# Attention scores of a transformer trunk: the distance term moves from a VectorE pass into TensorE's accumulation

## What is computed

```python
slopes = exp2(-8.0 * arange(1, 9) / 8)                     # one per head
dist = abs(qpos[:, None] - key_pos[None, :])
allowed = (key_pos[None, :] // 64) <= (qpos[:, None] // 64)
bias = where(allowed, -slopes[h] * dist, -inf)
s = einsum('bqhcd,bkhcd->bhcqk', q_blk, k)                 # 64 channels per map
p = softmax(s + bias, axis=-1)
a = p[:, :, 0] - lam_full * p[:, :, 1]
o = einsum('bhqk,bkhe->bqhe', a, v)
```

## Time and profile before

| | value |
|---|---|
| median of three executions | 1612.39 us |
| the profiled execution, its own time | 1613.23 us |
| its span, first to last instruction | 1611.4 us |
| mean granted TensorE clock over the span | 0.973 of full speed |
| head stage, first scores to the first matmul of the output projection | 132.07 to 168.89 us |

### The profile page before, as it was taken

How to read it: one execution, slowest core, us unless ns; L and a number is a source line. 1 busy time by engine, 2 the same in 40 slices (tenths; PEclk the granted TensorE clock), 3 DMA queues, 4 the chain that set the end, 5 groups by cost and what they waited for, 6 DMA issues and landing times.

```text
span 1611.4 us, 21780 instructions
## 1 busy us (share of the span) xinstructions
PE 1493.7 (93%) x9526; PEld 1091.1 (68%) x9526; DVE 472.5 (29%) x1003; ACT 161.5 (10%) x428; POOL 37.6 (2%) x84
## 2 busy tenths in 40 slices
PE   4997999999999899989999999999898899998997
PEld 3864587885477677443356887778683597886884
DVE  1577327351047455151211111111112311011113
ACT  2005210000020121021000000000000000000000
POOL 1000100000011100010000000000000000000000
PEclk8999999999999999999989999999999999999998
DMA  9996129859432110759998999999999999999995
GB/s 336 387 393 230 57 93 366 320 188 360 156 105 105 53 52 1 274 196 357 401 370 337 392 395 392 395 393 395 393 382 398 389 378 395 392 395 392 395 392 202
DMA packets 205824, 483.49 MB, mean 300 GB/s; under 512 B 4241, under 2 KB 6698, under 8 KB 205714
## 3 DMA queue, kind: packets, MB, share of 16 engines
q1 hardware_dynamic: 205106, 481.46, 79.9%
q10 hardware_dynamic: 608, 0.47, 0.1%
HBM read 480.86 MB, written 1.05 MB: 299 GB/s over the span
## 4 chain that ended last, share of the span: by engine, by line
PE 74%; DMA 13%; DVE 5%; SPq 4%; issue 3%; ACT 1%; POOL 0%; DVEq 0%; POOLq 0%
PE ps L1209 18%; PE ps L1729 15%; PE ps L1196 10%; DMA ring<-in_moe_w_gate 7%; PE ps L1787 7%; PE ps L1745 4%; PE ps L1585 3%; DMA ring<-in_moe_w_down 3%; DMA ring<-in_attn_w_in 3%; SPq L620 2%; PE ps L1752 2%; PE ps L1253 2%; PE ps L1635 2%; PE ps L1797 2%; SPq L617 1%
## 5 line engine op out<-in xcount | busy, mean ns | idle before, releaser
L1209 PE MATMUL ps<-hT,ring 128*128 128x256 f32 x1472 | 326.7, 382 | 5.1 <-issue 1.8
L1209 PEld LDWEIGHTS ps<-hT,ring 128*128 128x128 f32 x1472 | 278.6, 191 | 49.0 <-issue 6.5
L1729 PE MATMUL ps<-arena,ring 128*128 128x208 f32 (+1 forms) x1792 | 295.7, 327 | 6.7 <-DMA ring<-in_moe_w_gate 6.7
L1729 PEld LDWEIGHTS ps<-arena,ring 128*128 128x128 f32 x1792 | 292.8, 191 | 9.5 <-DMA ring<-in_moe_w_gate 9.0
L1196 PE MATMUL ps<-ring,arena 128*128 128x512 f32 x368 | 158.8, 592 | 1.3 <-DVE arena L2243 1.3
L1787 PE MATMUL ps<-arena,ring 128*128 128x208 f32 (+1 forms) x896 | 149.3, 327 | 2.6 <-DMA ring<-in_moe_w_down 2.6
L1787 PEld LDWEIGHTS ps<-arena,ring 128*128 128x128 f32 x896 | 145.2, 190 | 3.7 <-DMA ring<-in_moe_w_down 3.0
L1745 PE MATMUL ps<-ring,arena 128*32 128x256 f32 x1792 | 110.2, 401 | 30.6 <-issue 30.6
L1196 PEld LDWEIGHTS ps<-ring,arena 128*128 128x128 f32 x368 | 69.5, 190 | 87.2 <-issue 87.2
L1745 PEld LDWEIGHTS ps<-ring,arena 128*32 128x32 f32 x1792 | 62.7, 116 | 76.2 <-issue 46.1
L2034 DVE SCALAR_TENSOR_TENSOR arena<-ring,cond,arena 128x512 f32<-128x512 f32 x140 | 105.3, 752 | 5.0
(11 more groups left out here) (348 smaller groups left out, 1089.5 us busy)
## 6 DMA issues: line engine op xcount, KB each, us to landing
ring<-in_moe_w_down SPq DMA_DIRECT2D x56, 2048.0 KB, 19.3
ring<-in_moe_w_gate SPq DMA_DIRECT2D x55, 2048.0 KB, 19.4
ring<-in_moe_w_up SPq DMA_DIRECT2D x55, 2048.0 KB, 20.0
ring<-in_mod_w SPq DMA_DIRECT2D x24, 2048.0 KB, 17.0
ring<-in_mlstm_w_in SPq DMA_DIRECT2D x8, 2048.0 KB, 9.1
ring<-in_attn_w_in SPq DMA_DIRECT2D x6, 2048.0 KB, 19.9
ring<-in_ffn_w_gate SPq DMA_DIRECT2D x5, 2048.0 KB, 12.4
ring<-in_ffn_w_up SPq DMA_DIRECT2D x5, 2048.0 KB, 12.8
```

Source lines behind the costliest of these rows:

```text
L1209: ins = pe.matmul(dst, w[:, k, c * P:(c + 1) * P], hT[:, k, :], start=(k == 0), stop=(k == KT - 1))
L1729: ins = pe.matmul(dst, weights_in[:, k, ft * P:(ft + 1) * P], xq[:, k, BASE:BASE + w], start=(k == 0), stop=(k == KT - 1))
```

## The change

The slope matrices are built first: GpSimd multiplies the identity by -slope for each head, 8 matrices of 128 by 128 in the space of `mod_acc`. TensorE then adds the distance term itself: ahead of each score product it multiplies the head's diagonal slope matrix with `dist` (128 rows) into the same bank, and the score product accumulates on it. VectorE's pass L2205 is gone; the maxima are read from PSUM. ScalarE's exponentials read PSUM and write `probs`, and ScalarE counts the banks empty, one per map. `keep_busy` and the loops' order stay.

```diff
@@ pool_program
+            for h in range(HEADS):
+                pool.wait_ge(mod_summed, MOD_ENDS[1] - 1 + h // 4)
+                pool.tensor_scalar(slopes[:, h], ident[:], -(2.0 ** (-8.0 * (h + 1) / HEADS)), None, ALU.mult).then_inc(slopes_ready, 1)
@@ act_program
             def exps(h):
-                act.wait_ge(maxed, h + 1)
+                if h >= PROBS:
+                    act.wait_ge(aT_full, h - PROBS + 1)
                 b = h % 2
                 for c in range(2):
-                    for q in range(TT):
+                    act.wait_ge(maxed, 2 * h + c + 1)
+                    for q, r in enumerate((slice(0, P), slice(P, 3 * P))):
                         i = b * 4 + c * 2 + q
-                        p = probs[:, h % PROBS, c, 0:P] if q == 0 else probs[:, h % PROBS, c, P:3 * P]
-                        ins = act.activation(p, p, ACT.Exp, bias=nmax[:, i:i + 1], accum_out=psum_s[:, i:i + 1])
-                ins.then_inc(probs_ready, 1)
+                        ins = act.activation(probs[:, h % PROBS, c, r], ps[:, (FILLS["heads"] + 2 * h + c) % UB, r], ACT.Exp,
+                                             bias=nmax[:, i:i + 1], accum_out=psum_s[:, i:i + 1])
+                    ins.then_inc(u_free, 1)
@@ pe_program
             def scores(h):
+                pe.wait_ge(slopes_ready, h + 1)
                 for c in range(2):
                     b = bank()
                     r = slice(DA * c, DA * (c + 1))
-                    pe.matmul(b[:, 0:P], qT[r, h, 0:P], kT[r, h, 0:P], start=True, stop=True)
-                    pe.matmul(b[:, P:3 * P], qT[r, h, P:2 * P], kT[r, h, :], start=True, stop=True).then_inc(u_full, 1)
+                    pe.matmul(b[:, 0:P], slopes[:, h], dist[:, 0:P], start=True, stop=False)
+                    pe.matmul(b[:, 0:P], qT[r, h, 0:P], kT[r, h, 0:P], start=False, stop=True)
+                    pe.matmul(b[:, P:3 * P], slopes[:, h], dist[:, P:3 * P], start=True, stop=False)
+                    pe.matmul(b[:, P:3 * P], qT[r, h, P:2 * P], kT[r, h, :], start=False, stop=True).then_inc(u_full, 1)
@@ dve_program
-            def logits(h):
+            def maxima(h):
                 bb = h % 2
-                if h >= PROBS:
-                    dve.wait_ge(aT_full, h - PROBS + 1)
-                slope = 2.0 ** (-8.0 * (h + 1) / HEADS)
-                for c in range(2):
-                    emptied(dve.scalar_tensor_tensor(out=probs[:, h % PROBS, c], in0=dist, scalar=-slope, in1=full()[:, 0:384],
-                                                     op0=ALU.mult, op1=ALU.add))
-                dve.wait_ge(u_free, u.n)
                 for c in range(2):
                     i = bb * 4 + c * 2
-                    dve.tensor_reduce(nmax[:, i:i + 1], probs[:, h % PROBS, c, 0:P], AX_X, ALU.max, negate=True)
-                    ins = dve.tensor_reduce(nmax[:, i + 1:i + 2], probs[:, h % PROBS, c, P:3 * P], AX_X, ALU.max, negate=True)
-                ins.then_inc(maxed, 1)
+                    b = full()
+                    dve.tensor_reduce(nmax[:, i:i + 1], b[:, 0:P], AX_X, ALU.max, negate=True)
+                    dve.tensor_reduce(nmax[:, i + 1:i + 2], b[:, P:3 * P], AX_X, ALU.max, negate=True).then_inc(maxed, 1)
 
             def difference(h):
                 bb = h % 2
-                dve.wait_ge(probs_ready, h + 1)
+                dve.wait_ge(u_free, FILLS["heads"] + 2 * (h + 1))
```

More of the change, by code:

```diff
@@ L100 @@
 FILLS["attn"] = 1 + KT // 2
+FILLS["heads"] = FILLS["attn"] + 12
 FILLS["ffn"] = FILLS["attn"] + 12 + 2 * HEADS + 2 + KT // 2 + KT // 2
@@ L327, in trunk @@
         squared = [flat_h[:, D:D + 512], flat_h[:, D + 512:2 * D], mod_acc[:, 0], mod_acc[:, 1]]
+        slopes = mod_acc.rearrange("p b (h n) -> p (b h) n", n=P)
         mod_rows = area(P)
@@ L457, in trunk @@
         lam_ready = sem("lam_ready")
+        dist_ready = sem("dist_ready")
+        slopes_ready = sem("slopes_ready")
         maxed = sem("maxed")
-        probs_ready = sem("probs_ready")
         a_ready = sem("a_ready")
@@ L1294, in keep_busy @@
                     pe.matmul(dst[:, 0:3 * P], ident[:], vecs[:], start=True, stop=True)
+            pe.wait_ge(dist_ready, 1)
             scores(0)
@@ L2145, in dve_program @@
             dve.memset(dist[0:CHUNK, CHUNK:P], BIG)
-            link(dve.memset(dist[0:CHUNK, 2 * P + CHUNK:3 * P], BIG))
+            dve.memset(dist[0:CHUNK, 2 * P + CHUNK:3 * P], BIG).then_inc(dist_ready, 1)
+            dve.wait_ge(dist_ready, 1)
             for t in range(TT):
@@ L2197, in dve_program @@
                                           op0=ALU.add, op1=ALU.mult))
-            def logits(h):
+            assert u.n == FILLS["heads"], u.n
+            def maxima(h):
                 bb = h % 2
-                if h >= PROBS:
-                    dve.wait_ge(aT_full, h - PROBS + 1)
-                slope = 2.0 ** (-8.0 * (h + 1) / HEADS)
-                for c in range(2):
-                    emptied(dve.scalar_tensor_tensor(out=probs[:, h % PROBS, c], in0=dist, scalar=-slope, in1=full()[:, 0:384],
-                                                     op0=ALU.mult, op1=ALU.add))
-                dve.wait_ge(u_free, u.n)
                 for c in range(2):
                     i = bb * 4 + c * 2
-                    dve.tensor_reduce(nmax[:, i:i + 1], probs[:, h % PROBS, c, 0:P], AX_X, ALU.max, negate=True)
-                    ins = dve.tensor_reduce(nmax[:, i + 1:i + 2], probs[:, h % PROBS, c, P:3 * P], AX_X, ALU.max, negate=True)
-                ins.then_inc(maxed, 1)
+                    b = full()
+                    dve.tensor_reduce(nmax[:, i:i + 1], b[:, 0:P], AX_X, ALU.max, negate=True)
+                    dve.tensor_reduce(nmax[:, i + 1:i + 2], b[:, P:3 * P], AX_X, ALU.max, negate=True).then_inc(maxed, 1)
             def difference(h):
                 bb = h % 2
-                dve.wait_ge(probs_ready, h + 1)
+                dve.wait_ge(u_free, FILLS["heads"] + 2 * (h + 1))
                 link(dve.reciprocal(prec[:, bb * 4:bb * 4 + 4], psum_s[:, bb * 4:bb * 4 + 4]))
@@ L2247, in dve_program @@
                 if h < HEADS:
-                    logits(h)
+                    maxima(h)
                 else:
```

## The result

Over the first four executions of each kernel the changed one has a median of 1629.69 us (1626.70 to 1639.02) against 1612.77 us; the ratio is 1.0114, with a 95% interval of 1.0098 to 1.013. The forecast was 1625.4 us, so plus 0.81%. The direction and the place were right; the size was not. Set against the 1612.39 us the prediction started from, the ratio means 1630.8 us, just above the range of 1617 to 1630.

The account below looks back on a forecast made before the run. TensorE was to replace VectorE as the head stage's bound: scores 21.1, changes of shape 12.6, `keep_busy` 3.2, `turn` 1.65, `values` 2.7 us, then the tail; 13.0 us later, so 1625.4 us against the median, range 1617 to 1630.

Parts of the forecast that it names:

- What bounds the kernel: Head stage: VectorE sets 3.81 us a head before the change; TensorE becomes the bound after it, at 5.2 us.
- Price of a change of shape: TensorE, head stage: each change between 64 and 128 rows costs 0.2 us in both directions, 63 changes 12.6 us.
- rival of half the price: Head stage: half of each 0.2 us change is hidden, so 6.3 us go; delay 6.7, time 1619.1 us; chance 0.12.
- Cost of a head: TensorE, head stage: streaming 2.64, changes of shape 1.6, `turn` and `values` 1.0, together 5.2 us a head.
- Reads of PSUM: VectorE's maxima, head stage: 10 ns more each from PSUM than from SBUF, with 0 and 100 as the ends.
- Nothing: ScalarE, head stage: its new wait and the banks coming free one exponential later were to cost no time.
- keep_busy: Head stage: its 10 records, 3.3 us, covered by idle TensorE before, are on the path whole after the change.
- The sum: Head stage: TensorE's 41.25 us from 132.07 plus the tail put the projection at 182.1 us, 13.2 later; 13.0 taken.
- the clock: TensorE, head stage: with work without a pause, granted clock expected at 1.00 up to `scores(7)`.
- The rival was named: Head stage: gaps at changes of shape count as idleness, three heads run slow, 13 us more, 1638 us; chance 0.06.
- the tail: From `difference(6)` to the output projection: 6.7 us before, 6.3 kept; a low clock there adds up to 2 us.

Follow-up runs that it names:

- e7_tail_busy: Changed kernel with its 5 `keep_busy` products moved from the head stage's start to the gaps before `turn(6)` and `turn(7)`; five executions 1623.0 to 1626.1 us, one 1639.4.
- e1_again: The changed kernel run again unaltered, for its spread and another profile; ratio 1.0112 to the kernel before.
- e10_again_b: The changed kernel run again unaltered, to profile a longer execution; the profiled one took 1640.23 us.

## Why the prediction was wrong in size

*What bounds the kernel.* Right. VectorE's 3.81 us a head gave way to TensorE's.

*Price of a change of shape.* Right: 0.2 us from the earlier trace rows, measured 0.19 to 0.20 in both directions. The rival of half the price is out: pairs of records take 0.41 and 0.63, not 0.32 and 0.54. The Trainium skill (TensorEngine Tiling (Array Packing), Key Properties) has a drain and no time for it; the trace agrees that the start is late, by 0.10 us, and shows the second half beside it.

*Cost of a head.* 5.2 us forecast, 5.13 measured; the end of `scores(7)` 173.3 against 172.87 us.

*Reads of PSUM.* I took 10 ns more for a maximum; it was 5 to 10. The 62 cycles that the Trainium skill charges (VectorE: DVE Perf Modes, the section on the TRN2 errata) do not show in these reductions: 414 against 409 ns.

*ScalarE.* "Nothing" was short by a little. From the end of `scores(7)` to the projection I had 8.8 us and it took 9.9. `exps(7)` starts at 174.95 us though its maxima are ready at 173.5: ahead of it in ScalarE's queue stands `move_o(4)`, which waits for `values(4)`, and TensorE does those behind `scores(7)`. I had looked at what the new wait holds up, and not at what stands ahead of the exponentials now that scores come late.

*keep_busy.* Right: 3.3 us on the path forecast, 3.0 measured in `e7_tail_busy`. As for what it was good for, I had only its cost.

*The sum.* 13.2 worked out and 13.0 taken, 13.8 in the profile of 1626.70 us. For that execution the forecast of 1626.2 us was 0.5 off.

*The step that failed* is the clock, in two places of the sum. In the stage it was "now it has work without a pause, so I expect 1.00 up to `scores(7)`". In six of 18 executions the time is that of a fall, and the five of them that were profiled show it, 1.6 to 2.2 us after the first slope product, with records back to back. The rival was named, with its price (13 us for three heads, 1638) and its reason (gaps at changes of shape count as idleness). The price fits: the projection started 12.0 to 12.9 us later in four profiles, 14.1 in the one whose stage also began 1.3 us late, and the times were 1638.8 to 1644.8 us. Whether the reason holds is open. What was wrong is its chance of 0.06, and that it was set against the forecast as an alternative. It is one of two things that the same kernel does.

At the stage's end, the low clock was taken out of the tail (6.7 us became 6.3) and its price of up to 2 us put in the range alone. Of five profiles of usual executions three have it, one of the changed kernel and two with the gap filled, with the projection 1.1 to 1.5 us later.

The fall alone does not make the miss. The six long ones add 12 x 6 / 18 = 4 us to the mean of all. Without its one long execution the first run has a mean of 1628.7 us, still 16.1 above before where 13.0 was forecast, and `e1_again`, with no long one, has a ratio of 1.0112. The twelve usual executions have a median of 1629.7 us, 4.3 above the forecast of 1625.4. Of that, 0.8 is the stage (13.8 for 13.0), and 1.1 to 1.5 the low clock at its end where it occurs. The remainder, up to 2.5 us behind the stage in one profile, is of the size by which that part differs between profiles of all kernels here, and no cause special to this change was found.

What stays open: what the chip counts when it lowers the clock inside the alternation, how often it does, whether the idle time ahead takes part, and where the last 2 us of the usual executions arise.

## What to carry to other kernels

Before work is moved to TensorE, look at the shapes it will stand between: a product over 128 rows between products over 64 costs two changes of 0.2 us and takes the neighbour away that ran beside them. Group by shape, as the 384-column slope products do, and the loss of 1% shrinks to 0.1% (1.0012); what then turns it into a win of 0.1 to 0.2% is taking idle products off the path (0.999, and 0.9983 with ScalarE's order changed too). An engine that "is half idle" is so in its order of work; count its new load in that order, with what it holds up at the stage's end.

## What the runs showed of the hardware

- A change between 64-row and 128-row products cost 0.19 to 0.20 us at the 2.4 GHz level. At the 1.2 GHz level a pair of 128-column records behind a change took 0.72 us; at twice 0.21 without a change, the change costs 0.30 (`e10_again_b`).
- Matmul records without a pause did not keep TensorE's clock up. In five profiles it fell between 133.7 and 134.9 us and stood at 0.50 for 23.9 us, while records covered 24.00 of the 24 us from 134 to 158. Ahead of the first slope product the engine had been idle twice, for 0.62 and 0.33 us, and the fall came 1.6 to 2.2 us behind that product, in the alternation of shapes. The rise came 4.3 to 5.3 us into ten records of one shape. That these brought it is not shown: `e7_tail_busy` has none there, and its long execution is only 15 us above its others.
- One kernel can have two times. The changed kernel lay at 1626.7 to 1631.2 us in twelve executions and at 1638.8 to 1644.8 in six, on the same inputs; a single profile, or four executions, shows one of them by luck.
